# Expert token lists built for halves of the tokens on 128 partitions, 32 entries each, and their transposition moved ahead of the products that open the output sums

## The chip, the cores and the metric

One core of one Trainium2 chip runs the whole program. The metric is the device time of one execution in microseconds (us), taken as the median of several runs. The engines are TensorE (PE, with its weight loads PEld shown apart), VectorE (DVE), ScalarE (ACT), GpSimd (POOL) and SyncE (SP). DMA transfers are issued from SP's queue (all large weight loads) and from POOL's queue (gathers and small parameters), and all run on the same 16 DMA engines.

## What is computed

Two decoder layers over 272 tokens (16 meta tokens and 256 others) of width 1024, all in float32. Each layer is a mixer (sparse attention and retention) and then a mixture of experts. The change lies in the second part:

```python
top_idx = top_k(where(group_mask, sigmoid(x @ w_router) + bias), 8)     # 64 experts, 8 per token
gates   = scores[top_idx] / sum * 2.5
for each expert e, over the tokens that chose it:                      # no token may be dropped
    y += gate * ((silu(x @ w_gate[e]) * (x @ w_up[e])) @ w_down[e])     # 1024 -> 256 -> 1024
h = layer_norm(alpha * h + y + shared_expert(x))
```

In the second layer the meta tokens are no longer needed, so only the 256 others are routed. The inputs are drawn from a fixed seed, so that the routing is the same in every run.

## The kernel before

Tokens lie in three chunks (`CHUNKS`, line 30): 16 meta tokens, and two of 128 (tokens 16 to 143 and 144 to 271). Experts are worked on in 32 pairs (`PAIRS`). For each expert the kernel makes a list of at most `CAP` = 64 token numbers. A pair's two lists fill the 128 rows of one tile: four blocks of 32 rows, blocks 0 and 1 for the first expert and 2 and 3 for the second.

**Making the lists (DVE).** PE transposes the matrix `chosen` (token by expert, zeros and ones) into bank 4, and sums it over tokens into columns 448 to 511 of that bank (lines 976 to 982). DVE multiplies it with a falling number for each token (line 1754), giving `left`, 64 partitions by 272 columns. `first_lists` (line 1460) then takes the eight largest numbers of each row (line 1465) and strikes them out (line 1467), `CAP // 8` = 8 times. `repeat_lists` (line 1470) writes the list four times over into `quads`, since each token row lies in DRAM as four quarter rows of 256 values and 64 gates (`ROW` = 320 values, 1280 bytes). The largest of the 64 counts becomes `count_i`, which every engine reads.

**Turning them (PE).** `turn_lists` (line 556) transposes lists and quads with small matmuls into bank 7, and `read_lists` (line 1477) makes of them the row numbers `rank_i` and the numbers `idf`. A list's unused place gives a number beyond the table, and the gather skips it.

**The round.** `round_` exists on every engine. POOL issues four indirect gathers for each pair (line 1829), one for each block of 32 list places; partition 32q + s of the tile gets quarter q of the token in place s. DVE transposes them (line 1492), PE multiplies with the gate and up weights (line 599), ACT and DVE form the hidden values, PE multiplies with the down weights (line 629), and one pair later scatters the result into the open sums in banks 0 to 4 (line 575). The first gathers wait for `ids_ready`, and for the gates' copy in DRAM (SP, line 505).

**Weights.** A ring of six 2 MB slots holds gate, up and down weights of two pairs. SP loads each part into its slot (`load_pair`, line 442) as soon as the pair two before has used that slot. Pairs 0 and 1 are loaded during the mixer; the first slot that comes free in a round is that of the gate weights of pair 0. SP's loop runs from one round into the next without another wait.

**Further rounds.** `EXTRA` = 4. If `count_i` is over `CAP`, every engine goes through `round_` four more times, over all 32 pairs, with the weights loaded anew (SP line 513, PE line 1040, ACT line 1286, DVE line 1765, POOL line 1906). In each, DVE first makes the next lists from what is left in `left`.

**Around the lists on PE.** After the counts PE ends the shared expert's products (line 941, for the meta tokens line 944), opens the sums of chunks 1 and 2 with the identity times alpha (`open_sums`, line 996), waits for the scores and, in the first layer, for the sigmoid of the meta tokens' shared part (ACT, line 1268), and then turns the lists. `turn_hidden` (line 954) and the shared expert's down products (line 1010) follow, and then the round.

Of the kernel before, what the change touches and what calls it, by code (L numbers as in the profile page):

```python
# [9 lines left out]
ALU = mybir.AluOpType  # L10
# [6 lines left out]
META = 16  # L17
# [13 lines left out]
KEYS = [16, 144, 272]  # L31
CAP = 64
EXTRA = 4
ROUNDS = 1 + EXTRA
PAIRS = E // 2
# [124 lines left out]
def decoder_kernel(nc, a, out):  # L160
    ctx = ExitStack()
    with ctx:
# [47 lines left out]
        def carve(sizes):  # L210
            at, views = 0, {}
            for name, n in sizes:
# [33 lines left out]

        mo = carve([("xg", 2 * XG), ("xgT", 2 * 1024), ("y", 2 * 1024), ("selg", 2 * T), ("left", T),
                    ("gates", 192), ("logitT", T), ("score", 192),
                    ("biased", 192), ("best2", 192), ("grp", 24),
                    ("gt", 192), ("eq", 192), ("rank", 24), ("picked", 192), ("chosen", 192), ("tmp", 192),  # L250
                    ("gsum", 3), ("ginv", 3), ("cmax", 1), ("sg", 256), ("ha", 256), ("h", 256), ("h2", 256),
                    ("hid0", 256), ("quads", 256)])

# [276 lines left out]
        def _(pe):  # L530
# [25 lines left out]
            def turn_lists(l, r):  # L556

                hold_here(pe, quads_ready[l], r + 1)
                own = ident[0:64, 0:64].rearrange("p (q e) -> p e q", e=2)
                for e in range(2):  # L560
                    mm(bank[7][64 * e:64 * e + 64, 0:PAIRS], mo["list"][0:64, :], own[:, e, :], start=True, stop=True)
                for b in range(4):
                    last = mm(bank[7][:, PAIRS * (b + 1):PAIRS * (b + 2)], mo["quads"][0:64, 128 * (b % 2):128 * (b % 2) + 128],
                              own[:, b // 2, :], start=True, stop=True)
                last.then_inc(list_turned[l], 1)
# [86 lines left out]
            for l in range(DEPTH):  # L652
# [323 lines left out]
                for n in QUERIES[l]:  # L976
                    t0, w = CHUNKS[n]
                    pe.transpose(bank[4][0:64, t0:t0 + w], ch[0:w, n, :], ident[0:w, 0:w])
                for n in QUERIES[l]:
                    last = mm(bank[4][:, 448:512], k["ones"][0:CHUNKS[n][1], :], ch[0:CHUNKS[n][1], n, :],  # L980
                              start=(n == QUERIES[l][0]), stop=(n == 2))
                last.then_inc(chosen_turned, 1)
# [31 lines left out]
                pe.wait_ge(h_ready_tok, NORM[(l, 0)][2])  # L1014
                open_sums(1)
                open_sums(2)
                pe.wait_ge(score_ready, SCORED[l])
                if l == 0:
                    pe.wait_ge(shared_sig, SHARED[l][0])
                turn_lists(l, 0)  # L1020
                turn_hidden(1)
                turn_hidden(2)
# [270 lines left out]
        def _(dve):  # L1293
            steps = [0]

            def step(ins):

                steps[0] += 1
                ins.then_inc(dve_step, 1)
# [149 lines left out]

            def make_lists(l, r, j0=0, j1=CAP // 8):  # L1450

                left = mo["left"][0:64, FIRST[l]:T]
                for j in range(j0, j1):
                    eight = mo["list"][0:64, 8 * j:8 * j + 8]
                    dve.max(eight, left).then_inc(list_step[l], 1)
                    hold_here(dve, list_step[l], r * (CAP // 4) + 2 * j + 1)
                    dve.match_replace(left, eight, left, 0.0).then_inc(list_step[l], 1)
                    hold_here(dve, list_step[l], r * (CAP // 4) + 2 * j + 2)

            def first_lists(l):  # L1460

                left = mo["left"][0:64, FIRST[l]:T]
                for j in range(CAP // 8):
                    eight = mo["list"][0:64, 8 * j:8 * j + 8]
                    dve.max(eight, left).then_inc(list_step[l], 1)
                    dve.wait_ge(list_step[l], 2 * j + 1)
                    dve.match_replace(left, eight, left, 0.0).then_inc(list_step[l], 1)
                    dve.wait_ge(list_step[l], 2 * j + 2)

            def repeat_lists(l, r):  # L1470

                dve.wait_ge(list_step[l], r * (CAP // 4) + CAP // 4)
                dve.tensor_copy(mo["quads"][0:64, :].rearrange("p (h q s) -> p h q s", h=2, q=4),
                                mo["list"][0:64, :].rearrange("p (h s) -> p h s", h=2).unsqueeze(2).to_broadcast([64, 2, 4, 32]))\
                    .then_inc(quads_ready[l], 1)

# [73 lines left out]
            for l in range(DEPTH):  # L1550
# [135 lines left out]
                part = {n: s3[n][:, own_chunks, :] for n in s3}  # L1686
                cubes = {n: cube[n][:, own_chunks, :, :] for n in cube}
                dve.wait_ge(h_ready_tok, NORM[(l, 0)][2])
                dve.wait_ge(score_ready, SCORED[l])
# [48 lines left out]
                def shared_hidden(n):  # L1738
# [10 lines left out]
                    for o, _, u in parts:  # L1749
# [3 lines left out]
                dve.wait_ge(chosen_turned, l + 1)  # L1753
                dve.scalar_tensor_tensor(mo["left"][0:64, lo:T], bank[4][0:64, lo:T], -1.0, k["iota_t"][0:64, lo:T],
                                         ALU.mult, ALU.mult).then_inc(left_ready, 1)
                dve.wait_ge(left_ready, l + 1)
                first_lists(l)
                repeat_lists(l, 0)
                step(dve.tensor_reduce(mo["cmax"][0:1, :], bank[4][0:1, 448:512], AX, ALU.max))
                after_steps()  # L1760
# [178 lines left out]
```

## Time and profile before

| | |
|---|---|
| median of 3 runs | 1453.35 us (1451.62 to 1454.11) |
| the profiled execution | 1451.26 us, of which its span is 1449.4 us |
| PE busy / DVE busy / POOL busy | 1355.2 / 430.7 / 349.0 us |
| mean granted TensorE clock | 0.991 |
| moved by DMA | 475.41 MB, of which 442.73 MB from SP's queue |

The page gives the busy share of each engine in 40 slices, the chain of work that ended last, and groups of instructions by line. Each layer's round of experts shows as a long stretch in which the DMA row stands at 9 (from 217 us and from 938 us); the mixers lie in the stretches between. A line number in a row is one of the kernel before. In the DMA views q1 is SP's queue and q0 is POOL's, with packets, megabytes and share of the 16 engines' time.

### The profile page before, as it was taken

What the parts mean: (1) busy time and instruction counts of PE and PEld (TensorE: products, weight loads), DVE (VectorE), ACT (ScalarE), POOL (GpSimd) and SP (SyncE); (2) the same over time, 40 slices, a digit from 0 to 9 for tenths busy, and PEclk for the clock granted to TensorE, in tenths of its full rate; (3) what the DMA queues carried; (4) which work ended last, traced back from release to release, by engine and by line L of the source; (5) the groups of instructions that cost most, each with busy time, mean ns of one, the idle gap of its engine ahead of it and who ended that gap; (6) DMA issues with size and microseconds to landing.
All of it is one profiled execution on the core that took longest, in us unless ns stands there. A gap on an engine that the chain in (4) does not pass through costs nothing.

```text
span 1449.4 us, 20485 instructions
## 1 busy us (share of the span) xinstructions
PE 1355.2 (93%) x7932; PEld 704.0 (49%) x7932; DVE 430.7 (30%) x1277; ACT 219.7 (15%) x546; POOL 349.0 (24%) x369
## 2 busy tenths in 40 slices
PE   8999989999999999999989999899998988898897
PEld 5755545454444444444448555445544444444443
DVE  0443452322222222222154433522222222222223
ACT  1254210010010000100021542010100100001000
POOL 2032335232222222221000313332322222222200
PEclk9999999999999999999999999999999999999999
DMA  9722439999999999999874325399999999999993
GB/s 335 300 107 88 165 99 365 409 411 410 411 411 411 411 411 411 412 412 410 317 266 172 116 88 196 113 408 408 411 408 412 412 410 409 412 412 411 411 414 127
DMA packets 108182, 475.41 MB, mean 328 GB/s; under 512 B 16260, under 2 KB 22712, under 8 KB 75232
## 3 DMA queue, kind: packets, MB, share of 16 engines
q1 hardware_dynamic: 92960, 442.73, 76.7%
q0 software_dynamic: 15168, 32.01, 6.5%
q8 instruction: 28, 0.46, 0.1%
q14 instruction: 26, 0.21, 0.0%
HBM read 491.21 MB, written 3.75 MB: 341 GB/s over the span
## 4 chain that ended last, share of the span: by engine, by line
PE 47%; DMA 46%; DVE 3%; issue 1%; POOL 1%; ACT 1%; POOLq 0%; SPq 0%; DVEq 0%; ACTq 0%
DMA ring<-in_w_up_dram 46%; PE bank L599 14%; PE bank L671 6%; PE bank L682 5%; PE bank L629 4%; PE bank L575 4%; PE bank L898 3%; PE bank L793 1%; PE bank L941 1%; PE bank L774 1%; PE bank L674 1%; PE bank L548 1%; PE bank L1010 1%; PE bank L783 1%; PE bank L736 0%
## 5 line engine op out<-in xcount | busy, mean ns | idle before, releaser
L599 PE MATMUL bank<-ring,region 128*64 128x256 f32 x4096 | 463.7, 381 | 61.9 <-DMA ring<-in_w_up_dram 57.2
L1829 POOL DMA_INDIRECT region<-h_rows,rank_i x256 | 255.7, 999 | 694.1 <-DVE region L1497 558.8
L599 PEld LDWEIGHTS bank<-ring,region 128*64 128x64 f32 x4096 | 299.0, 137 | 245.3 <-DMA ring<-in_w_up_dram 77.5
L575 PE MATMUL bank<-region 128*128 128x512 f32 x512 | 247.2, 606 | 1.4 <-ACT region L1111 1.4
L629 PE MATMUL bank<-ring,region 128*64 128x512 f32 x1024 | 233.9, 599 | 0.0
L1530 DVE TENSOR_TENSOR region<-region,bank 128x256 f32<-128x256 f32 x64 | 27.0, 421 | 619.5 <-ACT region L1106 619.5
L1492 DVE STREAM_TRANSPOSE region<-region 128x256 f32<-128x256 f32 x256 | 141.7, 612 | 22.4 <-DMA region<-h_rows,rank_i 18.8
L629 PEld LDWEIGHTS bank<-ring,region 128*64 128x64 f32 x1024 | 67.9, 137 | 158.1 <-issue 109.6
L1111 ACT ACTIVATE region<-bank 128x512 f32<-128x512 f32 x128 | 76.4, 597 | 436.2 <-PE bank L629 436.2
L575 PEld LDWEIGHTS bank<-region 128*128 128x128 f32 x512 | 87.3, 190 | 89.1 <-issue 85.9
L1106 ACT ACTIVATE region<-bank 128x256 f32<-128x256 f32 x64 | 24.5, 383 | 486.5 <-PE bank L599 486.5
L671 PE MATMUL bank<-ring,hT 128*128 128x512 f32 x192 | 90.8, 621 | 2.5 <-ACT hT L1064 1.6
L682 PE MATMUL bank<-hT,ring 128*128 128x272 f32 (+2 forms) x320 | 73.6, 389 | 0.0
L682 PEld LDWEIGHTS bank<-hT,ring 128*128 128x128 f32 (+1 forms) x320 | 58.6, 186 | 12.5 <-issue 1.1
L1537 DVE COPY region<-bank 128x256 f32<-128x256 f32 x64 | 27.2, 424 | 124.9 <-PE bank L617 124.9
L671 PEld LDWEIGHTS bank<-ring,hT 128*128 128x128 f32 x192 | 37.0, 200 | 43.8 <-issue 42.2
L898 PE MATMUL bank<-ring,region 128*128 128x512 f32 x128 | 56.6, 595 | 0.0
L1806 POOL TENSOR_TENSOR ln_rstd<-ln_var,half_pow 128x1 f32<-128x1 f32 (+1 forms) x10 | 6.6, 657 | 173.5 <-DVE ln_var L1361 173.5
L1052 ACT ACTIVATE region<-bank 128x256 f32<-128x256 f32 (+6 forms) x58 | 21.1, 399 | 111.1 <-PE bank L682 51.2
L898 PEld LDWEIGHTS bank<-ring,region 128*128 128x128 f32 x128 | 23.8, 191 | 27.6 <-issue 27.6
L1865 POOL TENSOR_TENSOR region<-region,const 128x256 f32<-128x256 f32 (+1 forms) x12 | 8.7, 722 | 99.2 <-ACT region L1133 99.0
L617 PEld LDWEIGHTS bank<-const,region 128*128 128x128 f32 x128 | 15.5, 141 | 30.5 <-issue 30.5
(208 smaller groups left out, 827.4 us busy)
## 6 DMA issues: line engine op xcount, KB each, us to landing
ring<-in_w_gate_dram SPq DMA_DIRECT2D x64, 2048.0 KB, 28.1
ring<-in_w_up_dram SPq DMA_DIRECT2D x64, 2048.0 KB, 28.6
ring<-in_w_down_dram SPq DMA_DIRECT2D x64, 2048.0 KB, 26.8
ring<-in_w_in_dram SPq DMA_DIRECT2D x8, 2048.0 KB, 21.0
ring<-in_w_o_dram SPq DMA_DIRECT2D x4, 2048.0 KB, 12.5
ring<-in_w_in_dram SPq DMA_DIRECT2D x4, 1024.0 KB, 15.8
region<-h_rows,rank_i POOLq DMA_INDIRECT x256, 6.1
ln_par<-in_ln_g_dram POOLq DMA_DIRECT2D x4, 512.0 KB, 6.1
```

The costliest lines, as they stand in the source:

```text
L575: last = mm(bank[SUM_BANKS[n][half]][0:w, :], selg[:, u, t0:t0 + w], y_sb[:, u, half * 512:(half + 1) * 512], start=False, stop=stop, skip ...
L599: last = mm(bank[5][64 * e:64 * e + 64, part * F:(part + 1) * F], xgT[:, u, kk, 64 * e:64 * e + 64], w[:, e, kk, :], start=(kk == 0), stop ...
L629: last = mm(bank[6 + half][64 * e:64 * e + 64, :], mo["h2"][:, j * 128 + 64 * e:j * 128 + 64 * e + 64], w[:, e, j, half * 512:(half + 1) * ...
L671: last = mm(bank[b][0:w, :], hT[:, kk, t0:t0 + w], in_slot(s)[:, kk, :], start=(kk == 0), stop=(kk == KC - 1))
L682: last = mm(bank[PROJ_BANK[name]][0:width, 0:T - t0], in_slot(s)[:, kk, at:at + width], hT[:, kk, t0:T], start=(kk == 0), stop=(kk == KC - 1))
L898: last = mm(bank[OUT_BANKS[n][half]][0:w, :], mixT[kk][:, t0:t0 + w], wo[:, kk % 4, half * 512:(half + 1) * 512], start=(kk == 0), stop=(k ...
L1106: act.activation(mo["sg"], bank[5][:, 0:F], ACT.Sigmoid).then_inc(sig_ready[l], 1)
L1111: act.activation(y_sb[:, u, half * 512:(half + 1) * 512], bank[6 + half][:, :], ACT.Copy)\
L1492: last = dve.transpose(xgT[:, u, :, 32 * b:32 * b + 32], xg[:, u, b, 0:QUARTER].rearrange("s (p k) -> s k p", k=KC))
L1530: dve.tensor_tensor(mo["ha"], mo["sg"], bank[5][:, 0:F], ALU.mult).then_inc(ha_ready[l], 1)
L1537: dve.tensor_copy(mo["h2"], bank[7][:, 0:F]).then_inc(ht_ready[l], 1)
L1829: pool.indirect_dma_start(out=xg[:, u, b, :], out_offset=None, in_=h_rows, in_offset=bass.IndirectOffsetOnAxis(ap=rank_i[:, at:at + 1], ax ...
```

## The change

`CAP` becomes 32, and a list is made for each expert and each half of the tokens (`SPLIT` = 144: tokens 0 to 143 on partitions 0 to 63, the others on partitions 64 to 127). So `left` has 144 columns on 128 partitions, and four passes make all the lists. A pair's four blocks are now expert 0 first half, expert 0 second half, expert 1 first half, expert 1 second half. The counts are taken for each half, and the largest of the 128 is compared with 32. On PE the transposition of `chosen` becomes a plain matmul with the identity, so that chunk 2 can land on partitions 64 to 127, and `turn_lists` has eight products where it had six. It stands ahead of both `open_sums` in the first layer, and between them in the second.

```diff
-CAP = 64
+CAP = 32
+SPLIT = 144
@@ turn_lists
-                own = ident[0:64, 0:64].rearrange("p (q e) -> p e q", e=2)
-                for e in range(2):
-                    mm(bank[7][64 * e:64 * e + 64, 0:PAIRS], mo["list"][0:64, :], own[:, e, :], start=True, stop=True)
                 for b in range(4):
-                    last = mm(bank[7][:, PAIRS * (b + 1):PAIRS * (b + 2)], mo["quads"][0:64, 128 * (b % 2):128 * (b % 2) + 128],
-                              own[:, b // 2, :], start=True, stop=True)
+                    e, half = b // 2, b % 2
+                    own = ident[:, 64 * half:64 * half + 64].rearrange("p (q e) -> p e q", e=2)[:, e, :]
+                    mm(bank[7][32 * b:32 * b + 32, 0:PAIRS], mo["list"], own, start=True, stop=True)
+                    last = mm(bank[7][:, PAIRS * (b + 1):PAIRS * (b + 2)], mo["quads"], own, start=True, stop=True)
@@ PE, after the choice
                 for n in QUERIES[l]:
-                    t0, w = CHUNKS[n]
-                    pe.transpose(bank[4][0:64, t0:t0 + w], ch[0:w, n, :], ident[0:w, 0:w])
+                    w, at, c0 = CHUNKS[n][1], n // 2, 0 if n == 0 else META
+                    mm(bank[4][64 * at:64 * at + 64, c0:c0 + w], ch[0:w, n, :], ident[0:w, 0:w], start=True, stop=True)
                 for n in QUERIES[l]:
-                    last = mm(bank[4][:, 448:512], k["ones"][0:CHUNKS[n][1], :], ch[0:CHUNKS[n][1], n, :],
-                              start=(n == QUERIES[l][0]), stop=(n == 2))
+                    w, at = CHUNKS[n][1], n // 2
+                    last = mm(bank[4][:, 384 + 64 * at:448 + 64 * at], k["ones"][0:w, :], ch[0:w, n, :],
+                              start=(n in (QUERIES[l][0], 2)), stop=(n > 0))
@@ PE, ahead of the round
-                open_sums(1)
-                open_sums(2)
+                if l:
+                    open_sums(1)
                 pe.wait_ge(score_ready, SCORED[l])
                 if l == 0:
                     pe.wait_ge(shared_sig, SHARED[l][0])
                 turn_lists(l, 0)
+                if l == 0:
+                    open_sums(1)
+                open_sums(2)
@@ first_lists (make_lists alike)
-                left = mo["left"][0:64, FIRST[l]:T]
+                left = mo["left"][:, FIRST[l]:SPLIT]
                 for j in range(CAP // 8):
-                    eight = mo["list"][0:64, 8 * j:8 * j + 8]
+                    eight = mo["list"][:, 8 * j:8 * j + 8]
@@ repeat_lists
-                dve.tensor_copy(mo["quads"][0:64, :].rearrange("p (h q s) -> p h q s", h=2, q=4),
-                                mo["list"][0:64, :].rearrange("p (h s) -> p h s", h=2).unsqueeze(2).to_broadcast([64, 2, 4, 32]))\
-                    .then_inc(quads_ready[l], 1)
+                dve.tensor_copy(mo["quads"].rearrange("p (q s) -> p q s", q=4),
+                                mo["list"].unsqueeze(1).to_broadcast([128, 4, CAP])).then_inc(quads_ready[l], 1)
@@ DVE, ahead of and after the choice
+                if l == 0:
+                    step(dve.memset(mo["left"][64:128, 0:META], 0.0))
...
-                dve.scalar_tensor_tensor(mo["left"][0:64, lo:T], bank[4][0:64, lo:T], -1.0, k["iota_t"][0:64, lo:T],
+                dve.scalar_tensor_tensor(mo["left"][0:64, lo:SPLIT], bank[4][0:64, lo:SPLIT], -1.0, k["iota_t"][0:64, lo:SPLIT],
                                          ALU.mult, ALU.mult).then_inc(left_ready, 1)
-                dve.wait_ge(left_ready, l + 1)
+                dve.scalar_tensor_tensor(mo["left"][64:128, META:SPLIT], bank[4][64:128, META:SPLIT], -1.0,
+                                         k["iota_t"][64:128, SPLIT:T], ALU.mult, ALU.mult).then_inc(left_ready, 1)
+                dve.wait_ge(left_ready, l * 2 + 2)
...
-                step(dve.tensor_reduce(mo["cmax"][0:1, :], bank[4][0:1, 448:512], AX, ALU.max))
+                step(dve.tensor_reduce(mo["cmax"][0:1, :], bank[4][0:1, 384:512], AX, ALU.max))
```

The tiles `left` and `quads` shrink with it, and what lies behind them in `region` moves up.

## Rows read from the trace of the kernel before

**Rows 1.** The page: the span, and DMA busy tenths in 40 slices.
```profile
span 1449.4 us, 20485 instructions
...
DMA  9722439999999999999874325399999999999993
```
**Rows 2.** The page's chain of work that ended last, shares by line.
```profile
DMA ring<-in_w_up_dram 46%; PE bank L599 14%; PE bank L671 6%; PE bank L682 5%; PE bank L629 4%; PE bank L575 4%; PE bank L898 3%; PE bank L793 1%; PE bank L941 1%; PE bank L774 1%; PE bank L674 1%; PE bank L548 1%; PE bank L1010 1%; PE bank L783 1%; PE bank L736 0%
```
**Rows 3.** The chain in order of time, second layer's round: start, length, what.
```profile
946.74 6.91 PE bank L599 x64
...
961.09 6.91 PE bank L599 x64
...
1065.82 3.70 PE bank L599 x32
...
1098.85 3.70 PE bank L599 x32
```
**Rows 4.** The DMA view of 937.5 to 1424.55 us: queues, and gathers' landing.
```profile
q1 hardware_dynamic: 32057, 188.29, 95.2%
q0 software_dynamic: 5694, 9.83, 5.7%
...
region<-h_rows,rank_i POOLq DMA_INDIRECT x118, 6.1
```
**Rows 5.** POOL's queue around pair 26's gathers (1294 to 1301 us), and pair 30's (1359.5 to 1367.5).
```profile
q0 software_dynamic: 188, 0.17, 7.6%
...
q0 software_dynamic: 192, 0.47, 15.6%
```
**Rows 6.** The timeline on DVE, lists in both layers: start, length, engine, line.
```profile
194.17 0.43 DVE L1754 SCALAR_TENSOR_TENSOR region<-bank,const 64x272 f32<-64x272 f32 x1 [0.26 <-PE bank L980]
...
194.64 0.44 DVE L1465 MAX8 region<-region 64x8 f32<-64x272 f32 x1
...
195.64 0.44 DVE L1465 MAX8 region<-region 64x8 f32<-64x272 f32 x1
...
912.63 0.42 DVE L1465 MAX8 region<-region 64x8 f32<-64x256 f32 x1
...
913.59 0.42 DVE L1465 MAX8 region<-region 64x8 f32<-64x256 f32 x1
```
**Rows 7.** The timeline around the turn of the lists, PE and ACT, first layer.
```profile
198.76 0.55 ACT L1268 ACTIVATE region<-bank 16x128 f32<-16x128 f32 x2 [1.52 <-PE bank L944]
...
203.25 0.30 PE L561 MATMUL bank<-const,region 64*64 64x32 f32 x4 [0.99 <-DVE region L1473]
...
203.49 1.08 PE L563 MATMUL bank<-const,region 64*128 64x32 f32 x8
```
**Rows 8.** The chain in order of time, second layer, from the sums to the gates.
```profile
914.77 3.43 PE bank L996 x8
...
920.82 0.30 PE bank L561 x4
...
927.61 2.13 DMA region<-h_rows,rank_i
...
932.18 7.13 PE bank L599 x64
```
**Rows 9.** Busy time by window, end of the weights' stream; last three: clock, DMA, GB/s.
```profile
1412.00:1414.00 2.00, 2.00 (x16) 1.08 (x13) 0.10 (x1) 0.38 (x1) 0.00 (x0) 1.00 1.03 422
...
1422.00:1424.00 2.00, 2.00 (x22) 1.24 (x18) 0.00 (x0) 0.00 (x0) 0.00 (x0) 1.00 0.38 156
...
1427.00:1429.00 2.00, 2.00 (x14) 1.07 (x11) 0.21 (x1) 0.38 (x1) 0.00 (x0) 1.00 0.12 49
```
**Rows 10.** The timeline, last pair's down products of the second layer.
```profile
1432.05 3.65 PE L629 MATMUL bank<-ring,region 128*64 128x512 f32 x16
```
**Rows 11.** Busy time by window around the second layer's turn; columns as Rows 9.
```profile
919.30:922.70 3.40, 1.31 (x12) 1.19 (x12) 2.01 (x10) 0.00 (x0) 0.00 (x0) 0.97 0.00 0
922.70:929.50 6.80, 5.82 (x10) 2.67 (x11) 1.55 (x4) 0.77 (x2) 4.71 (x5) 0.51 0.16 42
```

More of the change, by code:

```diff
@@ L245, in decoder_kernel @@
         xhat = [region[:, at:at + 3072].rearrange("p (b n) -> p b n", b=3) for at in (9143, 9192)]
-        mo = carve([("xg", 2 * XG), ("xgT", 2 * 1024), ("y", 2 * 1024), ("selg", 2 * T), ("left", T),
+        mo = carve([("xg", 2 * XG), ("xgT", 2 * 1024), ("y", 2 * 1024), ("selg", 2 * T), ("left", SPLIT),
                     ("gates", 192), ("logitT", T), ("score", 192),
@@ L251, in decoder_kernel @@
                     ("gsum", 3), ("ginv", 3), ("cmax", 1), ("sg", 256), ("ha", 256), ("h", 256), ("h2", 256),
-                    ("hid0", 256), ("quads", 256)])
+                    ("hid0", 256), ("quads", 128)])
         mo.update({name: region[:, at:at + n] for name, at, n in
@@ L1448, in last_norm, with make_lists @@
                 scale(2)
-            def make_lists(l, r, j0=0, j1=CAP // 8):
-                left = mo["left"][0:64, FIRST[l]:T]
-                for j in range(j0, j1):
-                    eight = mo["list"][0:64, 8 * j:8 * j + 8]
+            def make_lists(l, r):
+                left = mo["left"][:, FIRST[l]:SPLIT]
+                for j in range(CAP // 8):
+                    eight = mo["list"][:, 8 * j:8 * j + 8]
                     dve.max(eight, left).then_inc(list_step[l], 1)
@@ L1460, in first_lists @@
             def first_lists(l):
-                left = mo["left"][0:64, FIRST[l]:T]
+                left = mo["left"][:, FIRST[l]:SPLIT]
                 for j in range(CAP // 8):
-                    eight = mo["list"][0:64, 8 * j:8 * j + 8]
+                    eight = mo["list"][:, 8 * j:8 * j + 8]
                     dve.max(eight, left).then_inc(list_step[l], 1)
```

## The prediction

> **What bounds the kernel now.** I read the DMA row of the page first: it stands at 9 in two long stretches, the rounds of experts [rows 1]. The chain of work that ended last agrees: 46% of the span is the landing of up weights [rows 2]. In order of time the second layer's chain shows two regimes [rows 3]. At the start of a round the ring is full and PE sets the pace: from 946.74 to 961.09, 14.35 us for a pair. Later PE waits for weights: the same step stands at 1065.82 and, two pairs on, at 1098.85, 16.5 us for a pair. So a round ends when the weights' stream ends, and the stream starts when the first slot comes free, behind the first gate products. Two questions follow for any change here: does it move that first step, and does it change what the DMA engines carry until the end.
>
> **The price of a pair of weights.** In 487.05 us, from the filling of the queues to the landing of the second layer's last up weights, SP's queue moved 188.29 MB, and POOL's 9.83 MB in 5.7% of the engines' time [rows 4]. A row of 1280 bytes thus costs 0.057 x 16 x 487.05 / 7680 = 0.058 us of one engine. These are 29.67 pairs. If the slowest engine carries 662 gathered rows (below), a pair of weights alone costs (487.05 - 38.4) / 29.67 = 15.1 us. The other way, 95.2% of the time for 29.9 pairs of 6.29 MB gives 15.5. I take 15.2, since gathers that skip every row still send small packets.
>
> **Whether the further rounds run.** This decides everything. Lists of 64 for all tokens become lists of 32 for half of them, and a single half list over 32 sends all engines through four more rounds. The trace of before can't show it, as it shows no second round. The routing can be counted, though, with the reference on its own inputs. First layer: the largest whole list has 58 tokens, the largest halves 31 and 27. Second layer: the largest whole list has 57, but expert 10 has 34 of its 56 tokens among 16 to 143; the largest second half has 26. 34 is over 32. Is it the routing of the chip? By the counts pair 26 gathers 136 rows (0.174 MB) and pair 30 gathers 368 (0.471 MB); the trace has 0.17 and 0.47 MB [rows 5]. I found the same for the other pairs that I looked at. Before, 57 was under 64 and no round was added; after, the second layer adds four, the first none (31).
>
> **The cost of the further rounds.** Each loads all 32 pairs again: 32 x 15.2 = 486.4 us, gathers next to nothing (two tokens in the first), and PE, at 14.35 us for a pair, is not the bound. Between rounds PE stops. From the end of the down products: copy and last sums about 4 us (eight passes took 3.43 [rows 8]), turn to first gates 932.18 - 920.82 = 11.4 us, with a gather that lands in 6.1 us under load [rows 4] rather than 2.13 [rows 8] 15.4, a longer turn 0.5, and half of the 7.13 us of gate and up products until a slot is free: about 23.5 us. SP doesn't wait for the round, so the stream goes on meanwhile. When the last up weights land (1424.55), seven loads of 5.07 us are still due, that pair's down and the next two pairs': 35.5 us. The down products end 11.15 us after it (1435.70 [rows 10]), so 24.3 us of stream are left. That covers the pause nearly. With PE at half clock after it the slot is freed up to 3.6 us later. I take 3 us of idle stream for a round, between 0 and 8. Four rounds: 4 x (486.4 + 3) = **1958 us** (1933 to 2016). The last normalisation must also wait for all four sums of the last round, about 2 us.
>
> **The lists.** DVE: a step of max and replace takes 1.00 us at 272 columns and 0.96 at 256 [rows 6], some 0.002 us a column, so 0.74 at 144 and 0.70 at 128. Four steps replace eight: 2.95 for 8.0 us, and 2.8 for 7.7. The second line 1754 adds 0.15 to the 0.47 us between 194.17 and 194.64; matmuls for transposes about 0.1; the memset falls into idle time ahead of the choice. The quads would be ready at 198.0 and 915.9. But PE takes work in order. In the first layer it waits for the sigmoid of line 1268, which ends at 199.3 [rows 7], so the turn starts there rather than at 203.25: 3.9 us earlier. In the second it stands behind half of the 3.43 us of opening products from 914.77 [rows 8]: 916.5 rather than 920.82, 4.3 earlier. The turn has 16 passes for 12; those of line 563 take 0.135 us each [rows 7], so 0.5 longer. The opening products moved behind it run while POOL issues gathers and DVE forms the hidden values, and delay only the shared part, which must be done by about 212 and 928 us. Gates' copies in DRAM are issued at 194 to 197 us, before the new gathers at 202.6. Together **-3.3 and -3.7 us**, and the stream of weights shifts with them.
>
> **The clock.** TensorE's granted clock was 0.97 in the stretch with PE busy for 1.31 of 3.40 us and then 0.51 for 6.8 us [rows 11]. The new order fills this hole, but in the second layer PE ends its shared products earlier and then waits some 3 us for the first gathered rows. If the clock falls there, half speed costs the first gate products up to 3.6 us, all of that layer's gain. [...] I keep the gain and put the loss in the range.
>
> **Where the gathered rows lie.** This is the second term, and it lies in the round. The tail of the stream shows how engines differ: all busy until 1412 to 1414, then a share of 0.38 (six of 16), and 0.12, two engines, alone from 1427 to 1429, with 49 GB/s [rows 9]. So two engines had more to carry, and others that are idle don't speed them up (49/2 and 422/16 are both about 25 GB/s). My reading: four neighbouring partitions share an engine, so places 0 to 3 of all blocks fall to two engines. Before, a list fills block 0 from the front and spills into block 1: in pairs 2 to 31 of the second layer these two carry 60 x 8 rows and 182 of the spill, 662; the mean is 484. After, each of 120 half lists of about 16 tokens fills its first places: 120 x 8 = 960 rows. The last places carry almost none. That is 298 rows or **+17 us** for the second layer, and 960 for 720, **+14 us**, for the first. The Trainium skill, "DMA: Bandwidth & Descriptors", section "The descriptor swizzle", gives that assignment of partitions to engines for a plain transfer to 128 partitions; the tail agrees, though no row names an engine. Were rows spread evenly, this term would be nothing.
>
> **The sum.** 1449.4 - 7 + 31 + 1958 + 2 = 3433.4; with the 1.9 us around the span 3435.3, and with the 2.1 us by which the median lies over the profiled execution **3437 us**.
>
> **The rivals.** (1) The rounds run, but the rows don't crowd on two engines: 3437 - 31 = 3406; for it that no row names an engine. (2) The pause between rounds isn't covered, because the ring stands empty at its start: 4 x 24 in place of 4 x 3, 3521; against it that SP's loop has no wait of its own. (3) The further rounds don't run, because the chip splits expert 10's tokens otherwise by two: 1453.35 - 7 + 31 = 1477. (4) The other side: neither rounds nor crowding, only the shorter lists: 1446, faster. It decides from a largest half list of 32 or less and rows spread evenly; against it stand the count of 34 and the tail.
>
> **Chances.** Forecast 0.76, (1) 0.12, (2) 0.05, (3) 0.04, (4) 0.03. About 0.2% is what a measurement can tell from no change. Slower 0.97; faster 0.02 and same 0.01 from (4), where half the gain may be lost to the clock. The range: 3385 (no crowding, 15.1 us for a pair, no idle stream) to 3500 (15.5 us, 8 us idle a round).
>
> **What would show it.** Right: line 599 with 32 pairs x 5 rounds + 32 = 192 pairs' products, SP's queue at some 1250 MB, DMA at 9 from about 934 us to the end; lines 1465 with four steps of 0.7 us; the turn near 199.3 and 916.5 us; the first layer's round longer by about 14 us. Wrong: about 7900 matmuls as before. If the first round of each layer keeps its length, the crowding was wrong; if the DMA row dips between rounds, the pause was.

## The result and the profile after

The changed kernel takes 3475.55 us (median of 4 runs, 3474.61 to 3476.84) beside 1453.73 us of the kernel before on the same chip: a ratio of 2.391, interval 2.387 to 2.396. The forecast was 3437 with a range of 3385 to 3500. The direction, the mechanism and the range held; the time came out 38.5 us above the forecast. The profiled execution's span is 3473.6 us.

The page of the kernel after (instruction counts; the DMA row in 40 slices; SP's queue; the gate and up products; the sums' products):

```profile
span 3473.6 us, 50442 instructions
...
DMA  7369999982499999999999999999999999999997
...
q1 hardware_dynamic: 230176, 1248.06, 89.7%
...
L599 PE MATMUL bank<-ring,region 128*64 128x256 f32 x12288 | 1402.2, 383 | 189.2 <-DMA ring<-in_w_up_dram 125.3
...
L575 PE MATMUL bank<-region 128*128 128x512 f32 x1536 | 741.2, 606 | 4.2 <-ACT region L1115 4.2
```

Line 599 runs 12288 times. A pair takes 64, so these are 192 pairs, six rounds of 32: one in the first layer and five in the second. SP's queue moves 1248.06 MB where it moved 442.73; the difference is 805.3 MB, or 4 x 32 pairs of 6.29 MB. The DMA row shows the two stretches of [rows 1] at its start, but the second one does not end.

The chain of work that ended last, in order of time, in the middle of the second layer's second round (start, length, what). This is the regime of [rows 3] in which PE waits for weights:

```profile
1761.67 3.70 PE bank L599 x32
...
1765.39 26.94 DMA ring<-in_w_up_dram
...
1792.37 3.70 PE bank L599 x32
```

Two pairs take 30.70 us here, 15.35 for one. The rate of the stream in this stretch gives the same price (length, then busy time of five engines; last three: granted clock, DMA share, GB/s):

```profile
1560.00:1920.00 360.00, 346.94 (x2159) 173.26 (x2157) 92.52 (x240) 37.50 (x71) 91.75 (x92) 1.00 1.02 410
```

A pair's 6.29 MB take 15.35 us at 410 GB/s. In the first rounds, with all tokens gathered, the same step takes 33.7 us on average; before it took 32.9.

The same view across the pause between the second and the third round of that layer:

```profile
1920.32 26.33 DMA ring<-in_w_up_dram
...
1954.22 3.61 PE bank L629 x16
...
1958.50 3.71 PE bank L575 x8
...
1963.46 0.22 PE bank L563 x2
...
1970.77 5.65 DMA region<-h_rows,rank_i
...
1978.68 9.09 PE bank L599 x64
```

The down products end at 1957.8. Then ACT copies their results, and PE adds the last sums, turns the lists, and waits for gathered rows until 1978.68. Then the gate and up products take 9.09 us, where the same 64 took 7.13 before [rows 8]. The timeline of SP shows when the first slot of the ring came free, and the windows show what the DMA engines did meanwhile (columns as above):

```profile
1984.49 0.38 SPq L453 DMA_DIRECT2D ring<-in_w_gate_dram  x1
```

```profile
1978.00:1979.00 1.00, 0.32 (x2) 0.29 (x4) 0.68 (x4) 0.00 (x0) 0.00 (x0) 0.50 0.89 320
1979.00:1980.00 1.00, 1.00 (x6) 0.47 (x4) 0.00 (x0) 0.00 (x0) 0.42 (x1) 0.50 0.40 152
...
1981.00:1985.00 4.00, 4.00 (x34) 2.41 (x32) 2.61 (x7) 0.00 (x0) 3.08 (x4) 0.80 0.04 6
1985.00:1986.00 1.00, 1.00 (x12) 0.68 (x10) 0.00 (x0) 0.00 (x0) 0.79 (x1) 1.00 0.96 123
```

The stream carries on through most of the pause and is dry for the last 5 us: the pause is covered, but not wholly. The clock stands at 0.50, the lower of its two levels, when the gate products begin.

The lists themselves, first layer, DVE's timeline and PE's. These lines answer [rows 6, 7]:

```profile
197.04 0.31 DVE L1469 MAX8 region<-region 128x8 f32<-128x144 f32 x1
197.79 0.31 DVE L1469 MAX8 region<-region 128x8 f32<-128x144 f32 x1
198.54 0.31 DVE L1469 MAX8 region<-region 128x8 f32<-128x144 f32 x1
199.28 0.31 DVE L1469 MAX8 region<-region 128x8 f32<-128x144 f32 x1
...
201.75 0.22 PE L563 MATMUL bank<-const,region 128*32 128x32 f32 x2 [0.91 <-issue]
```

There are four steps of 0.75 us instead of eight of 1.00. In the second layer they lie 0.72 us apart.

### The profile page after: what moved, and what is told of

It is laid out like the page before. It is cut to its first block, busy times and chain, and to the rows that moved or that the text cites. A ratio compares the mean times of both kernels' runs of the same rounds, so it can differ in the third digit from the quotient of the medians.

```text
span 3473.6 us, 50442 instructions
## 1 busy us (share of the span) xinstructions
PE 3238.3 (93%) x19529; PEld 1646.9 (47%) x19529; DVE 930.0 (27%) x2596; ACT 422.5 (12%) x930; POOL 859.6 (25%) x881
## 3 DMA queue, kind: packets, MB, share of 16 engines
q1 hardware_dynamic: 230176, 1248.06, 89.7%
## 4 chain that ended last, share of the span: by engine, by line
DMA 48%; PE 48%; DVE 1%; issue 1%; POOL 0%; ACT 0%; POOLq 0%; SPq 0%; DVEq 0%; ACTq 0%
DMA ring<-in_w_up_dram 48%; PE bank L599 22%; PE bank L575 8%; PE bank L629 8%; PE bank L671 3%; PE bank L682 2%; PE bank L898 1%; DMA region<-h_rows,rank_i 1%; PE bank L793 1%; PE bank L617 1%; PE bank L941 0%; PE bank L774 0%; DVE region L1495 0%; PE bank L674 0%; PE bank L549 0%
## 5 line engine op out<-in xcount | busy, mean ns | idle before, releaser
L599 PE MATMUL bank<-ring,region 128*64 128x256 f32 x12288 | 1402.2, 383 | 189.2 <-DMA ring<-in_w_up_dram 125.3
L1836 POOL DMA_INDIRECT region<-h_rows,rank_i x768 | 766.4, 998 | 2202.4 <-DVE region L1500 1630.1
L599 PEld LDWEIGHTS bank<-ring,region 128*64 128x64 f32 x12288 | 892.1, 138 | 750.6 <-DMA ring<-in_w_up_dram 177.4
L575 PE MATMUL bank<-region 128*128 128x512 f32 x1536 | 741.2, 606 | 4.2 <-ACT region L1115 4.2
L629 PE MATMUL bank<-ring,region 128*64 128x512 f32 x3072 | 703.2, 600 | 2.1 <-DVE region L1540 2.1
L1533 DVE TENSOR_TENSOR region<-region,bank 128x256 f32<-128x256 f32 x192 | 80.9, 421 | 1804.4 <-ACT region L1110 1804.4
L1495 DVE STREAM_TRANSPOSE region<-region 128x256 f32<-128x256 f32 x768 | 425.5, 611 | 99.2 <-DMA region<-h_rows,rank_i 70.1
L629 PEld LDWEIGHTS bank<-ring,region 128*64 128x64 f32 x3072 | 203.9, 137 | 475.7 <-issue 330.2
L575 PEld LDWEIGHTS bank<-region 128*128 128x128 f32 x1536 | 261.5, 190 | 267.6 <-issue 258.1
L1115 ACT ACTIVATE region<-bank 128x512 f32<-128x512 f32 x384 | 229.3, 597 | 1258.5 <-PE bank L629 1258.5
L1538 DVE TENSOR_TENSOR region<-region,bank 128x256 f32<-128x256 f32 x192 | 80.8, 421 | 25.4
L1529 DVE TENSOR_SCALAR region<-const,region 128x256 f32<-128x256 f32 (+1 forms) x192 | 79.1, 412 | 3.1 <-PE bank L575 3.1
```

The source lines that it names most:

```text
L575: last = mm(bank[SUM_BANKS[n][half]][0:w, :], selg[:, u, t0:t0 + w], y_sb[:, u, half * 512:(half + 1) * 512], start=False, stop=stop, skip ...
L599: last = mm(bank[5][64 * e:64 * e + 64, part * F:(part + 1) * F], xgT[:, u, kk, 64 * e:64 * e + 64], w[:, e, kk, :], start=(kk == 0), stop ...
L629: last = mm(bank[6 + half][64 * e:64 * e + 64, :], mo["h2"][:, j * 128 + 64 * e:j * 128 + 64 * e + 64], w[:, e, j, half * 512:(half + 1) * ...
L1115: act.activation(y_sb[:, u, half * 512:(half + 1) * 512], bank[6 + half][:, :], ACT.Copy)\
L1495: last = dve.transpose(xgT[:, u, :, 32 * b:32 * b + 32], xg[:, u, b, 0:QUARTER].rearrange("s (p k) -> s k p", k=KC))
L1533: dve.tensor_tensor(mo["ha"], mo["sg"], bank[5][:, 0:F], ALU.mult).then_inc(ha_ready[l], 1)
```

## Where the 2024 us lie

The two profiled spans differ by 3473.6 - 1449.4 = 2024.2 us. The landing of the last up weights of a round splits this into three parts.

- Up to that landing in the second layer's first round: 1447.92 after, 1424.55 before, **+23.4 us**.
- From there over four further rounds to the last landing, 1447.92 to 3444.72: **+1996.8 us**, 499.2 a round.
- From the last landing to the end: 28.9 us for 24.85, **+4.0 us**.

The sum of the prediction had 24, 1958 and 2 in these places. So the further rounds hold nearly all of the miss: 38.8 of 40.2 us. The first part agrees in total, but by errors that cancel. Against the kernel before, `chosen` is written 2.1 us later in the first layer of this execution (194.36 for 192.26), the lists give back 2.8 and 2.5 us, the streams of the two layers take 11.0 and 13.1 us longer, and the low clock costs 2.5. That adds up to the 23.4. The forecast had 31 for the streams, 7 for the lists, and nothing for the other two.

## Experiments

**The further rounds alone.** On all five engines the comparison becomes

```diff
-                with pe.If(most > CAP):
+                with pe.If(most > 2 * CAP):
```

> The changed kernel, with the further rounds entered only from a count over 64, so the second layer has one round; the last two of expert 10's 34 tokens of the first half are left out of the output. The theory (the four rounds cost 4 x 500 us; in the first round of each layer the gathered rows crowd on two DMA engines, 960 rows each in pairs 2 to 31 for 720 and 662 before; 11 and 13 us more; the shorter lists give back 5 us) expects 1473 us, between 1468 and 1480. The rival that rows don't crowd, and that the whole 2022 us come from the rounds, expects 1448. A pair in the stretch with PE waiting for weights: 16.8 us by the theory, 16.4 by the rival.

It took 1474.75 us (1472.92 to 1477.72), ratio 1.0142, interval 1.0127 to 1.0157; before on this chip 1454.23. So the further rounds cost 2000.8 us of the 2021.8. What is left of the change is still slower than before, by 20.5 us: shorter lists and an earlier turn bring less than something else takes.

**One further round in place of four.**

```diff
-EXTRA = 4
+EXTRA = 1
```

> The changed kernel with EXTRA = 1, one further round in place of four (lists of 64 for each half in all, enough for every token here). The trace of the changed kernel has its further rounds 499.3 to 500.5 us apart, so three less expect 3475.6 - 3 x 499.7 = 1976.5 us. The rival, that the first further round costs more or less than the others (it starts with the DMA engines out of step after the crowded round), expects the time to differ from that by more than 3 us.

It took 1990.69 us (1988.73 to 1992.49) beside 1468.61 of before on its chip: 522.1 us more, where 522.7 was expected. Line 599 ran 6144 times, 96 pairs. The recorded 1976.5 us is missed by 14 us, since it was worked out from runs on another chip: the kernel before takes 14.4 us more on this one. Beside it, little of the rounds' price is paid once only: each costs about half a millisecond.

**The rows' places.** The lists are unchanged, but each block starts at another place, so that the filled places of the four blocks fall to different DMA engines by the reading of the prediction. The quads get a fifth copy, and each block's products read from an offset:

```diff
+TURN = [0, 4, 6, 2]
...
-                    mm(bank[7][32 * b:32 * b + 32, 0:PAIRS], mo["list"], own, start=True, stop=True)
-                    last = mm(bank[7][:, PAIRS * (b + 1):PAIRS * (b + 2)], mo["quads"], own, start=True, stop=True)
+                    at = 4 * TURN[b]
+                    mm(bank[7][32 * b:32 * b + 32, 0:PAIRS], mo["quads"][:, at:at + 32], own, start=True, stop=True)
+                    places = mo["quads"][:, at:at + 128]
+                    last = mm(bank[7][:, PAIRS * (b + 1):PAIRS * (b + 2)], places, own, start=True, stop=True)
```

> As e1_no_rounds (the same two tokens left out), but the places of the four lists of a pair are turned by 0, 16, 24 and 8 of 32, so that the first tokens of each lie on other DMA engines: by the reference's counts the fullest engine carries 604 and 566 rows in pairs 2 to 31 in place of 960 and 960. The count of rows, of instructions on POOL and PE, and the rounds stay; DVE copies five repeats in place of four. Crowding at 0.058 us a row expects 43 us less than e1_no_rounds, 1430; at the 0.045 that the traces of before and after give, 34 less, 1440. The rival (rows don't matter, something else in the first rounds became slower) expects the time of e1_no_rounds within 2 us.

It took 1441.45 us (1439.72 to 1444.32), ratio 0.9924, interval 0.9909 to 0.9938: 33.3 us less than without the offsets. The windows at the end of the stream, columns as above, without offsets:

```profile
1440.00:1444.00 4.00, 4.00 (x12) 1.51 (x12) 1.53 (x4) 0.26 (x1) 0.00 (x0) 1.00 0.54 222
1444.00:1448.00 4.00, 4.00 (x26) 1.68 (x24) 0.15 (x1) 1.19 (x2) 0.00 (x0) 1.00 0.39 162
1448.00:1452.00 4.00, 3.61 (x36) 2.14 (x34) 0.00 (x0) 0.00 (x0) 0.00 (x0) 1.00 0.33 137
1452.00:1456.00 4.00, 4.00 (x29) 2.22 (x26) 0.62 (x2) 0.38 (x1) 0.00 (x0) 1.00 0.16 63
```

and with them:

```profile
1408.00:1412.00 4.00, 4.00 (x36) 2.37 (x34) 0.00 (x0) 0.67 (x2) 0.00 (x0) 1.00 0.86 346
1412.00:1414.00 2.00, 1.49 (x16) 0.75 (x14) 0.00 (x0) 0.00 (x0) 0.00 (x0) 1.00 0.49 203
1414.00:1416.00 2.00, 2.00 (x22) 1.35 (x20) 0.00 (x0) 0.00 (x0) 0.00 (x0) 1.00 0.37 152
1416.00:1418.00 2.00, 2.00 (x11) 0.86 (x8) 0.63 (x2) 0.38 (x1) 0.00 (x0) 1.00 0.19 78
```

Without offsets the share of busy engines decays over more than 12 us, from about half to a sixth. With them it drops within about 6. The same bytes move, and the offsets change only which partitions they fill. This is the test of the crowding: rival 1, rounds but no crowding, falls. The two executions also differ outside the stream, so the stream by itself, from the first free slot to the start of the last 32 gate and up products, is the better measure. The table takes in the next experiment:

| | first layer | second layer |
|---|---|---|
| half lists, no further rounds | 506.19 us | 501.42 us |
| the same with offsets | 490.88 us | 484.72 us |
| kernel before | 495.10 us | 488.55 us |
| the same with offsets | 487.92 us | 483.40 us |

By it the offsets give 32.0 us for 960 - 604 + 960 - 566 = 750 fewer rows on the fullest engine, 0.043 us a row.

**The same places in the kernel before.** Lists of 64 for all tokens, with offsets for the four blocks:

```diff
+TURN = [0, 4, 2, 3]
...
-                for e in range(2):
-                    mm(bank[7][64 * e:64 * e + 64, 0:PAIRS], mo["list"][0:64, :], own[:, e, :], start=True, stop=True)
                 for b in range(4):
-                    last = mm(bank[7][:, PAIRS * (b + 1):PAIRS * (b + 2)], mo["quads"][0:64, 128 * (b % 2):128 * (b % 2) + 128],
-                              own[:, b // 2, :], start=True, stop=True)
+                    at = 160 * (b % 2) + 4 * TURN[b]
+                    places = mo["quads"][0:64, at:at + 128]
+                    mm(bank[7][32 * b:32 * b + 32, 0:PAIRS], places[:, 0:32], own[:, b // 2, :], start=True, stop=True)
+                    last = mm(bank[7][:, PAIRS * (b + 1):PAIRS * (b + 2)], places, own[:, b // 2, :], start=True, stop=True)
```

> The kernel before, with lists of 64, its places turned in the same way (0, 16, 8 and 12 of 32), nothing else: the fullest engine carries 562 and 522 rows in place of 720 and 662. Crowding expects 298 rows x 0.045 to 0.058 us, 13 to 17 us less than before, near 1439, the turn of the lists 0.3 us dearer. If crowding began only with half lists (the rival: before was bound by the mean of the engines), it expects 1454.

It took 1445.31 us (1442.81 to 1448.09), ratio 0.995, interval 0.9936 to 0.9964: 8.9 us faster, where 13 to 17 were expected. The sign is right, the size is not. By the count of rows the fullest engine has 720 - 562 + 662 - 522 = 298 fewer. The streams are 12.3 us shorter, by the table above, so a row is worth 0.041 us here too. The rest of the miss lies ahead of the streams, in the profiled executions: counted from the write of `chosen` the gate products start 0.9 and 1.2 us later than before, where 0.3 was allowed for the dearer turn, and `chosen` itself is written 2.0 us later in the first layer (194.31 for 192.26).

**The order of the turn alone**, in the kernel before:

```diff
-                open_sums(1)
-                open_sums(2)
+                if l:
+                    open_sums(1)
                 pe.wait_ge(score_ready, SCORED[l])
...
                 turn_lists(l, 0)
+                if l == 0:
+                    open_sums(1)
+                open_sums(2)
```

> The kernel before with one part of the change alone: the turn of the lists stands ahead of both openings of the sums in the first layer and between them in the second. PE had ended the openings about 1 and 2.6 us before the lists were ready, so the turn can't start earlier. The theory (the order alone gives nothing, it pays only with the shorter lists) expects no change, within 1 us. The rival: the opening products now fill PE's idle time behind the turn, the clock stays up, and the gates start 1 us earlier or, if they get in the way of the shared part, 1 to 3 us later in a layer.

It took 1454.08 us, ratio 1.0005, interval 0.9995 to 1.0014: no difference. With the long lists the turn waits for DVE anyway [rows 7], and its place before the opening products is worth nothing. In the trace PE is idle for 4.6 and 4.3 us ahead of it, the turn takes 2.3 us for 1.3, and the gate products start 0.9 us later after the write of `chosen` in each layer. So what the starts gain needs the shorter lists. The shorter lists in the old order weren't run, so the share of each isn't known.

**Half lists that fit.** The whole change, with the offsets, and with the second layer cut at token 128 rather than 144, so that its parts are tokens 16 to 127 and 128 to 271. The largest part of expert 10 then has 30 tokens, the largest list of all 31, and no further round runs. Nothing is left out:

```diff
+                if l:
+                    mm(bank[4][0:64, 16:128], ch[:, 1, :], ident[:, 0:112], start=True, stop=True)
+                    mm(bank[4][64:128, 0:16], ch[:, 1, :], ident[:, 112:128], start=True, stop=True)
+                    mm(bank[4][64:128, 16:144], ch[:, 2, :], ident, start=True, stop=True)
...
+                end, c0 = (SPLIT, META) if l == 0 else (128, 0)
```

> The whole change and its condition, but with the second layer's tokens split at 128 in place of 144, so that the largest half list has 30 tokens (the first layer keeps 144, with 31), and with the places turned as in e2_no_rounds_spread. No token is left out and no threshold is changed. The theory (the count over 32 and the crowding are all that was wrong with the change) expects the time of e2_no_rounds_spread and 0 to 2 us for two more products and masks: 1442. The rival, that leaving out two tokens or the test's place made e2_no_rounds_spread fast, expects it over 1450.

It took 1456.64 us (1455.32 to 1460.75) beside 1468.61 of before on its chip: ratio 0.9927, interval 0.9908 to 0.9946. This beats both kernels and agrees with the 0.9924 of the kernel that left two tokens out. The recorded 1442 us is missed by 14.6 us, by as much as the kernel before is slower on this chip; read as ratios, the expectation holds and its rival falls. Two tokens of one expert separate it from the 3475 us.

**The clock after the wait, second layer.** Without further rounds; while PE waits for the first gathered rows it works on five idle products:

```diff
+                if l:
+                    for _ in range(5):
+                        mm(bank[7][:, :], ident, k["decay"][:, 0:512], start=True, stop=True)
                 hold_here(pe, count_ready, l + 1)
```

> As e1_no_rounds (two tokens left out), with five idle products of 128x512 on PE (10 passes, 4.3 us) in the second layer behind the shared part, in PE's 4.5 us of idle time ahead of the first gates; their results are never read. In e1_no_rounds the first 64 gate and up products took 9.86 us there at half clock, against 7.13 at full. The theory expects 7.1 us, and the stream of weights and the end 2 to 3 us earlier, 1472. The rival, that the clock didn't set the start of the stream, expects the time of e1_no_rounds, 1474.8, within 1 us.

The first run, ratio 1.0145 (interval 1.0123 to 1.0168), stood beside no kernel without the idle products on its chip, and it showed gaps in line 599 that the traces of the first experiments lack (last section). It settled nothing, so both went on one chip:

> The kernel with the comparison against 64, so without further rounds (two tokens of expert 10 in the second layer are left out), once more, beside the version with the clock held. 1475 us (1471 to 1479), the second layer's first 64 gate and up products taking 9.6 to 9.9 us.

> The same without further rounds (two tokens left out), with five idle products in the second layer while TensorE waits for the first gathered rows. Theory (the low clock costs the first slot 2.5 us, and the stream shifts with it): 2.5 us less than r_e1_no_rounds, first gate products 7.1 us. Rival (something else holds the first products, such as gaps in which TensorE waits for nothing that the profile shows): no difference, and the gaps stand in the rows of line 599.

1476.31 us (1474.86 to 1477.4) without the idle products and 1471.03 (1469.76 to 1475.04) with them: 5.3 us less. The timelines of PE and SP, first without:

```profile
942.14 9.96 PE L599 MATMUL bank<-ring,region 128*64 128x256 f32 x64 [4.50 <-DVE region L1495]
...
948.84 0.40 SPq L453 DMA_DIRECT2D ring<-in_w_gate_dram  x1
```

and with:

```profile
939.28 7.13 PE L599 MATMUL bank<-ring,region 128*64 128x256 f32 x64 [0.20 <-DVE region L1498]
...
943.15 0.40 SPq L453 DMA_DIRECT2D ring<-in_w_gate_dram  x1
```

From the first gate product to the first free slot 6.70 us pass without and 3.87 with. So the low clock costs 2.8 us, and that is as expected. The rest isn't what the experiment was for: in this execution the gate products already began 2.86 us earlier, as the lists' turn before them did (926.40 for 929.25). Without the idle products the clock stood at 0.50 in two more stretches of the second layer's mixer, ahead of the edit; with them it was up there:

```profile
811.40:814.80 3.40, 3.40 (x10) 1.91 (x9) 3.09 (x15) 1.94 (x6) 0.00 (x0) 0.50 0.61 258
866.00:869.40 3.40, 3.40 (x14) 1.00 (x15) 1.12 (x2) 1.28 (x2) 1.86 (x2) 0.50 0.08 29
```

Why it fell there in one kernel and not in the other is open.

**The clock in the pauses.** Fourteen idle products behind the turn of each further round:

```diff
                         turn_lists(l, r)
+                        for _ in range(14):
+                            mm(bank[6][:, :], ident, k["decay"][:, 0:512], start=True, stop=True)
                         round_(l, r)
```

> The changed kernel with 14 idle products of 128x512 on PE (28 passes, 12 us) behind the turn of the lists in every further round, in the 13 us in which PE waits for the first gathered rows. Their results are never read. The theory: the stream of weights runs dry for some 6.5 us between rounds, of which 2 us come from the first gate products at half clock (first slot free 5.8 us after they start, against 3.9); so 2 us less a round, 8 less in all, 3467, and no stretch at half clock when the gates start. The rival: the stream isn't waiting for that slot, and the time stays within 2 us, or grows if the products get in the way.

The first run gave 3504.54 us, ratio 2.3874 (2.382 to 2.3928), which can't be told from the 2.391 of the changed kernel. The pair on one chip:

> The changed kernel once more, beside its version with the pause filled, so that both are read on one chip. 3470 to 3490 us; in each further round TensorE's clock is low over the first gate products (9.1 to 10.1 us for the first 64), and the first slot of the ring comes free 5.8 us after they start.

> The changed kernel with 14 idle products behind the lists' turn in each further round, beside the unchanged one on the same chip. Theory (the low clock lengthens each pause by some 2 us, since the first slot comes free later): 4 x 2 = 8 us less than r_after. Rival (the clock falls all the same, a few microseconds later, because TensorE soon waits for the next pair's rows): no difference, within 3 us. The low stretch of the granted clock, where it lies and for how long, tells them apart.

3474.18 us (3472.47 to 3478.54) unchanged, 3471.01 (3469.77 to 3471.37) with idle products: 3.2 us less, neither 8 nor nothing. The timelines say why. Two pauses with idle products:

```profile
1965.32 15.00 PE L1050 MATMUL bank<-const 128*128 128x512 f32 x28
...
1984.13 0.38 SPq L453 DMA_DIRECT2D ring<-in_w_gate_dram  x1
...
2464.23 12.26 PE L1050 MATMUL bank<-const 128*128 128x512 f32 x28
...
2481.49 0.38 SPq L453 DMA_DIRECT2D ring<-in_w_gate_dram  x1
```

and the first slots of the unchanged kernel on the same chip:

```profile
1983.84 0.38 SPq L453 DMA_DIRECT2D ring<-in_w_gate_dram  x1
...
2484.40 0.38 SPq L453 DMA_DIRECT2D ring<-in_w_gate_dram  x1
```

In all four rounds the clock is up when the gate products begin, and the slot comes free 3.9 us after them, for 5.3 to 6.4 in the unchanged kernel. In the first of the two pauses shown the idle products run at the low clock at first, take 15.0 us and delay the gates' start to 1980.26, which was 1978.59: the gain is spent there. In the second they take 12.26 us and end in time, and from slot to slot 497.4 us pass, where the unchanged kernel takes 500.6. Over all four further rounds, from the start of the last 32 gate and up products of one round to that four rounds on, 1989.8 us pass with idle products and 1995.7 without, 5.8 less; the first rounds, which the edit doesn't touch, end 1.4 us later in that execution. The rival, that the clock falls a little later all the same, is seen once here, for 3.4 us from 2984.6, and in all four further rounds of the first run's trace (from 1499.5, for example), each time behind the first 64 products, which had taken 7.13 us.

## Why the prediction held, and where its sizes were off

**Whether the rounds run.** Right, with 192 pairs. The one count of 34 decided a factor of 2.4. The higher threshold and the other split each take the further rounds away, and with them some 2000 us. Rivals 3 and 4 fall with it. Rival 4 was close all the same: without further rounds and without crowding the kernel is 0.73% faster than before.

**The price of a round.** The step that was mis-sized, 499.2 us for 489.4. Half of it is the pair: 15.35 us, not 15.2, makes 32 x 0.15 = 4.8 us. I had two estimates, 15.1 and 15.5, and took a value near the lower one. The lower one rested on 0.058 us for a gathered row; at the 0.041 to 0.044 measured since, the same division gives 15.4 to 15.5, near the measured price. The other half is the idle stream: 499.2 - 32 x 15.35 = 8.0 us, not 3. Three things made it longer. The slot came free 26.7 us after the down products, not 23.5; of this the low clock is 1.9 (5.81 us from the first gate product to the slot, for 3.87 with the clock up). The loads still due covered about 21.7 us of it, not 24.3: the stream runs dry around 1979.5. These two leave 5.0 us dry. The other 3 lie at the edges, for which I had no term: from 1978 to 1980 the stream moves 236 GB/s and from 1986 to 1988 303, where the full rate is 410. For the cover I multiplied seven loads by the mean time of one, though several are under way at once (one takes 25 to 27 us from issue to landing). That this is the whole reason was not tested. My range for the idle stream, 0 to 8, just held it. Both ends of the stated range were added up wrongly: their terms give 3381 and 3495, not 3385 and 3500. The measured time lies inside both.

**Rival 2, an uncovered pause**, asked for 24 us idle in each. The DMA share is 0.89 still at 1978, when the pause is 20 us old, so it falls.

**The crowding.** Right in kind, high in size. First layer: from the first gate product to the landing of pair 29's up weights 684.15 - 215.37 = 468.8 us before, and after 694.44 - 214.69 = 479.8: +11.0 us where +14 was forecast. In the second layer, from the first free slot to the last landing: 501.65 for 488.51, +13.1 for +17. With 240 and 298 more rows that is 0.046 and 0.044 us a row, and the offsets gave 0.043 and 0.041. So a row costs nearly the same in all three comparisons. The 0.058 was a queue's busy share divided by all its rows; that share also holds the small packets of skipped rows, and why it overstates the delay was not tested.

**The lists and the turn.** The four steps came out at 0.75 and 0.72 us for the 0.74 and 0.70 expected. Counted from the write of `chosen`, the gate products start 20.33 us later in the first layer, 23.11 before: 2.8 us gained for 3.3 expected. The turn of 16 passes takes 2.1 us, 0.75 longer instead of 0.5. Second layer: 19.86 for 22.40, 2.5 gained for 3.7.

**The clock.** I kept the gain and put the loss in the range; the loss came. In the second layer 6.33 us pass from the first gate product to the first free slot, 3.86 before. That is 2.5 us, all that the lists had gained. With the shorter lists and the new order together PE is idle for 4.5 us ahead of the gates (the order alone left 2.2), the clock stands at 0.50 for 6.8 us from 938.1, and the idle products show that the clock is the cause. The Trainium skill, "TensorE: Matmul & The Clock Gate", section "Why this matters for your kernels", warns of idle gaps between bursts of matmuls; these rows agree. The same loss returns in each further round. There the 3 us of idle stream were meant to hold it.

**The last sums.** +4.0 us for +2. Line 575 now has all its eight passes ahead of the first statistics (3.71 us at 3456.57), where before four were enough (2.00 us). That is 1.7 of it. Two statistics follow one after the other behind them (1.31 us) where one did (0.71), which makes 2.4 with the gaps. The other 1.6 lie behind the last instruction of DVE, from whose end 4.6 us pass to the end of the span, for 3.0 before; their cause is open.

## What to carry to other kernels

When a change makes a fixed capacity smaller, count the real load against it first: one overfull list decides more than every saving of the shorter lists. When list entries decide which partitions a gather fills, count the rows that each DMA engine gets, for the fullest one ends last; starting each block at another place cost nothing in the kernel with half lists and gave 33 us. And price a pause by the moment at which a slot is free again, with the clock that stands then, against loads that overlap.

## What the runs showed of the hardware

- Which partitions a gather fills sets the time, at equal bytes: 33.3 us between two kernels of which one has 960 rows of 1280 bytes on its fullest engine in each layer, by my count, and the other 604 and 566. Within the streams that is 0.043 us a row, and 0.041 in the kernel before. The Trainium skill, "DMA: Bandwidth & Descriptors", section "The descriptor swizzle", gives the assignment for plain transfers; the runs agree that gathers follow it, though no row names an engine.
- After a wait of 4.5 to 13 us PE's first 64 products took 8.5 to 10.1 us for 7.1, at a granted clock of 0.50 at first. Products that compute nothing, run during the wait, restore the 7.13 us.
- On one of the chips line 599 stopped again and again in the first pairs, for nothing that the profile names: 16.5 us in 18 gaps, against 0.2 and 0.3 us in the changed kernel's two traces, taken elsewhere. The rows are PE's waits (total, times, longest), first of the kernel with one further round, then of the changed kernel:

```profile
PE bank L599 <- issue: 16.5, 18, 1.6
```

```profile
PE bank L599 <- issue: 0.3, 2, 0.2
```

All four kernels of that chip have such gaps, 9.7 to 16.5 us, and the kernel before took 14.4 us longer there than on the chip of the first experiments. That the gaps are this difference is likely but not shown, and their cause is open.
